# First units of a layer on unscaled x, their eviction scaled, and low halves moved to VectorE

## Time and profile before

| | |
|---|---|
| median of 3 runs | 1706.01 us (1705.09 to 1707.49) |
| the profiled execution | 1704.73 us |
| its span, first to last instruction | 1702.9 us |
| mean granted TensorE clock | 0.975 |
| TensorE busy | 1593.6 us, 94% |
| VectorE busy | 934.9 us, 55% |
| ScalarE busy | 855.7 us, 50% |
| GpSimd busy | 741.6 us, 44% |
| HBM traffic | 140 GB/s over the span |

### The profile page before, as it was taken

The page is one execution under the profiler, slowest core; times in us unless marked ns, Lnnn a source line. Parts: engine busy times, 40 slices in busy tenths (PEclk is TensorE's granted clock), DMA queues, the critical chain, the costliest instruction groups (busy, mean ns, idle before and its releaser), DMA issues.

```text
span 1702.9 us, 28287 instructions
## 1 busy us (share of the span) xinstructions
PE 1593.6 (94%) x10947; PEld 1454.9 (85%) x10947; DVE 934.9 (55%) x2023; ACT 855.7 (50%) x1526; POOL 741.6 (44%) x572
## 2 busy tenths in 40 slices
PE   4999878999999989999899988899999999889998
PEld 3888778998788989999888878898887778889998
DVE  3799965444565554444379998423035545633332
ACT  2577764553455444444357776443325646444442
POOL 0688853332222424444258895365411112334432
PEclk8999989999999999999999999999999999999999
DMA  4654435446553546766444434675752112646654
GB/s 127 143 146 135 130 108 175 133 165 127 122 123 124 163 135 177 195 175 197 124 124 137 136 128 138 152 186 140 182 153 71 51 56 86 194 136 177 187 156 125
DMA packets 341453, 240.11 MB, mean 141 GB/s; under 512 B 36925, under 2 KB 328475, under 8 KB 341320
## 3 DMA queue, kind: packets, MB, share of 16 engines
q1 hardware_dynamic: 329880, 231.33, 47.7%
q10 hardware_dynamic: 10992, 6.29, 1.7%
q0 software_dynamic: 448, 0.69, 0.5%
HBM read 236.55 MB, written 1.74 MB: 140 GB/s over the span
## 4 chain that ended last, share of the span: by engine, by line
PE 70%; DVE 17%; ACT 5%; issue 4%; POOL 2%; DMA 1%; SPq 1%; DVEq 0%; POOLq 0%; ACTq 0%
PE bank L598 8%; DVE bank L876 8%; PE bank L599 8%; PE bank L600 8%; PE bank L634 4%; PE bank L636 4%; PE bank L635 4%; PE bank L990 4%; PE bank L1288 3%; PE bank L596 3%; PE bank L1289 3%; PE bank L1290 3%; PE bank L610 2%; DVE wlo L371 2%; PE bank L1083 1%
## 5 line engine op out<-in xcount | busy, mean ns | idle before, releaser
L371 POOL TENSOR_TENSOR wlo<-ring,whi 128x1024 fp32r<-128x1024 f32 (+3 forms) x210 | 481.7, 2295 | 786.0 <-ACT whi L362 785.9
L362 ACT CAST whi<-ring 128x1024 fp32r<-128x1024 f32 (+4 forms) x389 | 379.2, 990 | 274.8 <-PE bank L600 106.2
L598 PE MATMUL bank<-xh,whi 128*128 128x256 f32 x1384 | 402.4, 291 | 32.4 <-DVE xl L562 19.4
L371 DVE TENSOR_TENSOR wlo<-ring,whi 128x1024 fp32r<-128x1024 f32 (+3 forms) x179 | 254.6, 1423 | 267.0 <-ACT whi L362 266.1
L599 PE MATMUL bank<-xl,whi 128*128 128x256 f32 x1384 | 397.0, 287 | 0.0
L600 PE MATMUL bank<-xh,wlo 128*128 128x256 f32 x1384 | 396.7, 287 | 0.0
L598 PEld LDWEIGHTS bank<-xh,whi 128*128 128x128 f32 x1384 | 271.2, 196 | 42.3 <-issue 39.8
L599 PEld LDWEIGHTS bank<-xl,whi 128*128 128x128 f32 x1384 | 271.6, 196 | 0.2
L600 PEld LDWEIGHTS bank<-xh,wlo 128*128 128x128 f32 x1384 | 271.2, 196 | 0.0
L819 POOL TENSOR_TENSOR scratch<-scratch 128x256 f32<-128x256 f32 x288 | 211.3, 766 | 127.0 <-ACT scratch L764 123.1
L596 PE MATMUL bank<-sqb,ring 128*128 128x256 f32 x1024 | 230.1, 385 | 17.3 <-DVE xl L562 9.7
(11 more groups left out here) (254 smaller groups left out, 2640.5 us busy)
## 6 DMA issues: line engine op xcount, KB each, us to landing
ring<-in_a_w_in_dram SPq DMA_DIRECT2D x64, 512.0 KB, 5.2
ring<-in_b_w_in_dram SPq DMA_DIRECT2D x32, 1024.0 KB, 5.8
ring<-in_c_w_in_dram SPq DMA_DIRECT2D x64, 512.0 KB, 5.4
ring<-in_w_in_dram SPq DMA_DIRECT2D x26, 1024.0 KB, 5.4
ring<-in_w_ffn_in_dram SPq DMA_DIRECT2D x44, 512.0 KB, 5.1
ring<-in_a_w_in_dram SPq DMA_DIRECT2D x16, 1024.0 KB, 5.3
ring<-in_a_w_out_dram SPq DMA_DIRECT2D x16, 1024.0 KB, 5.0
ring<-in_w_ffn_out_dram SPq DMA_DIRECT2D x16, 704.0 KB, 4.5
```

Source lines behind the costliest of these rows:

```text
L362: nc.scalar.copy(piece(whi, h)[:, :, 0:n], src).then_inc(hi_done, 1)
L371: engine.tensor_tensor(piece(wlo, h)[:, :, 0:n], src, piece(whi, h)[:, :, 0:n].bitcast(F32), ALU.subtract).then_inc(done, 1)
L598: nc.tensor.matmul(o, wh[:, k, :], xh[:, k, :], start=(k == 0), stop=False)
```

## The change

In each layer the first two projection units (in the forgetting attention the gate unit and the first quarter of query and key) are multiplied by x times gain, without the factor of the norm. ScalarE writes these halves (`raw_high`) for each group of x as soon as it is added, VectorE the low halves (`raw_low`), and `proj_raw` does the products, with the last sum of squares inside the first unit or behind it. VectorE multiplies the two banks by `rr` when it evicts them (`raw_scale`); later steps read that copy. The normalised `sqb`, `xh` and `xl` are made later, `xh` and `xl` over the unscaled ones when TensorE has read these (`norm_dve_all`, `norm_high`, `norm_low`), and the third unit waits for them. In the conformer layers GpSimd makes `sqb` from a copy `xg`, the first two val and gate units are no longer plain, and the first z unit is the first to need the normalised halves. The order of the first steps on VectorE and ScalarE changes with it. VectorE gets all low halves but those of z, of the first half of the conformer output, of the mixer projections from the third on, of the branches and the mix gates. At the very start ScalarE waits for the gains before its first weight halves.

```diff
-                halves.append((u, ap, k, n, dve and len(halves) % 2 == 0))
+                halves.append((u, ap, k, n, dve == ALL or (dve and len(halves) % 2 == 0)))
...
-        def plan_out(w, nk):
-
-            return [(kb, g, unit_in(w[kb * D:(kb + 1) * D, :], [(2 * g * P, 2 * P)], True))
+        def plan_out(w, nk, dve="all"):
+
+            return [(kb, g, unit_in(w[kb * D:(kb + 1) * D, :], [(2 * g * P, 2 * P)], dve if kb == 0 else ALL))
                     for kb in range(nk // KD) for g in range(4)]
 
...
+        def raw_high(act, ph, g):
+
+            act.wait_ge(x_done, 4 * ph + g + 1)
+            for k in (2 * g, 2 * g + 1):
+                if ph in (0, 3):
+                    nc.scalar.activation(xg[:, k, :], xT[:, k, :], ACT.Identity, scale=norm_g(GAIN[ph], k)).then_inc(xg_done, 1)
+                nc.scalar.activation(xh[:, k, :], xT[:, k, :], ACT.Identity, scale=norm_g(GAIN[ph], k)).then_inc(rh_done, 1)
+
+        def raw_low(dve, ph, g):
+            for k in (2 * g, 2 * g + 1):
+                dve.wait_ge(rh_done, KD * ph + k + 1)
+                nc.vector.scalar_tensor_tensor(xl[:, k, :], xT[:, k, :], norm_g(GAIN[ph], k), xh[:, k, :].bitcast(F32),
+                                               ALU.mult, ALU.subtract).then_inc(rl_done, 1)
+
+        def rr_both():
+            return rr[:, 0:S].unsqueeze(1).to_broadcast((P, 2, S))
...
         def rms_act(act, ph):
             for g in range(0 if ph == 0 else 3, 4):
+                raw_high(act, ph, g)
                 rms_square(act, ph, g)
             act.wait_ge(ss_done, ph + 1)
             nc.scalar.activation(std[:, 0:S], rms_bank[ph][:, 0:S], ACT.Sqrt, scale=1.0 / D, bias=eps).then_inc(std_done, 1)
-            for g in range(4):
-                act.wait_ge(xr_done, KD * ph + 2 * g + 2)
-                nc.scalar.copy(xh[:, 2 * g:2 * g + 2, :], sqb[:, 2 * g:2 * g + 2, :]).then_inc(xh_done, 1)
+
+        def norm_high(act, ph, g, u):
+
+            act.wait_ge(xr_done, KD * ph + 2 * g + 2)
+            if ph == 1:
+                act.wait_ge(half_done, u + 2 * g + 2)
+            elif g < 3:
+                act.wait_ge(raw_used, RAW_USED[ph] + g + 1)
+            else:
+                group_done(act, u)
+            nc.scalar.copy(xh[:, 2 * g:2 * g + 2, :], sqb[:, 2 * g:2 * g + 2, :]).then_inc(xh_done, 1)
+
+        def norm_low(dve, ph, g):
+            dve.wait_ge(xh_done, 4 * ph + g + 1)
+            nc.vector.tensor_tensor(xl[:, 2 * g:2 * g + 2, :], sqb[:, 2 * g:2 * g + 2, :],
+                                    xh[:, 2 * g:2 * g + 2, :].bitcast(F32), ALU.subtract).then_inc(xn_done, 1)
...
-        def rms_dve(dve, ph):
+        def rms_dve(dve, ph, lo=-1):
+            for g in range(0 if ph == 0 else 3, 4):
+                raw_low(dve, ph, g)
+            lo_dve_to(dve, lo)
             dve.wait_ge(std_done, ph + 1)
             nc.vector.reciprocal(rr[:, 0:S], std[:, 0:S]).then_inc(rr_done, 1)
             dve.wait_ge(rr_done, ph + 1)
-            def low(g):
-                dve.wait_ge(xh_done, 4 * ph + g + 1)
-                nc.vector.tensor_tensor(xl[:, 2 * g:2 * g + 2, :], sqb[:, 2 * g:2 * g + 2, :],
-                                        xh[:, 2 * g:2 * g + 2, :].bitcast(F32), ALU.subtract).then_inc(xn_done, 1)
-
+
+        def norm_dve_all(dve, ph):
             for k in range(KD):
                 nc.vector.scalar_tensor_tensor(sqb[:, k, :], xT[:, k, :], norm_g(GAIN[ph], k), rr[:, 0:S],
                                                ALU.mult, ALU.mult).then_inc(xr_done, 1)
-                if k % 2 == 1 and k >= 3:
-                    low(k // 2 - 1)
-            low(3)
+
+        def raw_scale(dve, ph, i, g, u, to):
+
+            group_done(dve, u)
+            nc.vector.tensor_tensor(to.rearrange("p (a t) -> p a t", t=S), bank[g % 2][:, :].rearrange("p (a t) -> p a t", t=S),
+                                    rr_both(), ALU.mult).then_inc(raw_ev, 1)
+
+        def raw_wait(eng, ph, i):
+            eng.wait_ge(raw_ev, RAW_EV[ph] + i + 1)
+
+        def proj_raw(pe, g, u, ph, opens=False, ends=False):
+
+            b = take_bank(pe, g)
+            for a, h in enumerate(hs(u)):
+                o = b[:, a * S:(a + 1) * S]
+                split_ready(pe, h)
+                wh, wl = piece(whi, h), piece(wlo, h)
+                for k in range(KD):
+                    if opens and a == 0:
+                        pe.wait_ge(rl_done, KD * ph + k + 1)
+                    nc.tensor.matmul(o, wh[:, k, :], xh[:, k, :], start=(k == 0), stop=False)
+                    nc.tensor.matmul(o, wh[:, k, :], xl[:, k, :], start=False, stop=False)
+                    mm = nc.tensor.matmul(o, wl[:, k, :], xh[:, k, :], start=False, stop=(k == KD - 1))
+                    if ends and h == last(u) and k in (1, 3, 5):
+                        mm.then_inc(raw_used, 1)
+                    if opens and a == 0 and k == KD - 3 and ph and len(hs(u)) > 1:
+                        rms_pe(pe, ph)
+                mm.then_inc(half_done, 1)
+                if opens and a == 0 and not (ph and len(hs(u)) > 1):
+                    rms_pe(pe, ph)
...
                 if kb == end:
+                    if g >= 1:
+                        raw_low(dve, n["ph"] + 1, g - 1)
                     group_done(dve, u)
...
+            pool.wait_ge(rr_done, n["ph"] + 1)
+            for k in range(KD):
+                pool.wait_ge(xg_done, KD * j + k + 1)
+                nc.gpsimd.tensor_tensor(sqb[:, k, :], xg[:, k, :], rr[:, 0:S], ALU.mult).then_inc(xr_done, 1)
...
+                        if c == 0 and k == TAPS_DVE // 4:
+                            raw_scale(dve, n["ph"], 1, *n["vg"][1], rawt(1))
...
+                if c == 1:
+                    for g in range(4):
+                        norm_low(dve, n["ph"], g)
...
+            g, u = n["f"]
+            dve_ahead(dve, u)
+            group_done(dve, u)
+            nc.vector.tensor_tensor(fw[:, 1, :], bank[g % 2][0:FH, 0:S], rr[0:FH, 0:S], ALU.mult).then_inc(raw_ev, 1)
+            norm_dve_all(dve, n["ph"])
...
                 dve_ahead(dve, u)
-                dve.wait_ge(c_cg, c + 1)
-                nc.vector.tensor_tensor(cup[:, c % 2, 2:S + 2], bank[g % 2][:, 0:S], ccg[:, c % 2, :], ALU.mult).then_inc(c_cu, 1)
+                if c:
+                    dve.wait_ge(c_cg, c)
+                    uu, cc = bank[g % 2][:, 0:S], ccg[:, c % 2, :]
+                else:
+                    raw_scale(dve, n["ph"], 0, g, u, craw[0])
+                    norm_dve_all(dve, n["ph"])
+                    raw_wait(dve, n["ph"], 0)
+                    uu, cc = craw[0][:, 0:S], craw[0][:, S:2 * S]
+                nc.vector.tensor_tensor(cup[:, c % 2, 2:S + 2], uu, cc, ALU.mult).then_inc(c_cu, 1)
...
                 dve_ahead(dve, u)
+                bb = bank[g % 2]
+                if c == 0:
+                    for i in range(4):
+                        norm_low(dve, n["ph"], i)
+                    raw_scale(dve, n["ph"], 1, g, u, craw[1])
+                    bb = craw[1]
...
+            lo_dve_to(dve, last(n["in"][1][2]))
+            for i in range(2):
+                _, g, u = n["in"][i]
+                if i == 1:
+                    norm_dve_all(dve, n["ph"])
+                group_done(dve, u)
+                nc.vector.tensor_tensor(qk[:, RAW_OF[i], :, :], bank[g % 2][:, :].rearrange("p (a t) -> p a t", t=S),
+                                        rr_both(), ALU.mult).then_inc(m_ev, 1)
+            for r in range(4):
+                norm_low(dve, n["ph"], r)
...
                 dve_ahead(dve, u)
+                src = bank[g % 2]
+                if i == 1:
+                    norm_dve_all(dve, n["ph"])
+                    for r in range(4):
+                        norm_low(dve, n["ph"], r)
+                if i < 2:
+                    raw_scale(dve, n["ph"], i, g, u, craw[i])
+                    src = craw[i]
                 dve.wait_ge(h_silu, i + 1)
-                nc.vector.tensor_tensor(y_slot(dve, n["y0"] + i), bank[g % 2][:, S:2 * S], sg[:, i % 2, :], ALU.mult).then_inc(y_raw, 1)
...
             act.wait_ge(set_pool, 1)
+            act.wait_ge(set_used, 1)
```

More of the change, by code:

```diff
@@ L290, in program @@
         first_half = []
+        ALL = "all"
         def cut(u, by_columns, dve, plain=False, rows_of=None):
@@ L428, in plan_conf @@
             for c in range(KE):
-                n["vg"].append((group((u_done, j * KE + c + 1)), unit_in(w, [(c * P, P), (E + c * P, P)], plain=True)))
+                n["vg"].append((group((u_done, j * KE + c + 1)), unit_in(w, [(c * P, P), (E + c * P, P)], c < 2 and ALL, plain=(c >= 2))))
                 if c % 4 == 3:
@@ L514, in plan_ffn @@
             n = {"ph": ph}
-            n["gu"] = [(group((y_raw, 64 + i + 1)), unit_in(w, [(i * P, P), (FF + i * P, P)], True)) for i in range(KF)]
+            n["gu"] = [(group((y_raw, 64 + i + 1)), unit_in(w, [(i * P, P), (FF + i * P, P)], ALL)) for i in range(KF)]
```

(10 more changed lines are left out.)

186 lines of the change are left out of this document (127 added, 59 removed).

## The result

The changed kernel takes 1714.53 us (median of 4 runs, 1711.99 to 1715.51). Against the kernel before the ratio is 1.0047, with a 95% interval of 1.0031 to 1.0063: some 8 us slower, where 12.4 us faster was forecast. The profiled execution took 1714.64 us.

The account below looks back on a forecast made before the run. TensorE, busy 94% of 1702.9 us, was taken to bound the kernel, VectorE's order setting the first conformer layer's pace. Terms 2.3 + 2.8 + 3.1 + 6.4 + 1.5 - 3.7 = 12.4 us off 1706.0 gave 1693.6, range 1684 to 1701.

Parts of the forecast that it names:

- The starts: Start of every layer: TensorE goes on with unscaled x times gain, no wait 2 to 7 us after the previous layer's outputs.
- What came late next: New waits: 4.7 us before unit 2 in the short layer, 4.1 in the feed-forward, 4.2 before L1288 in the forgetting layer.
- the short layer: Short convolution: unit 2 starts 18.2 instead of 21.3 us after the previous layer's last output matmul; less 0.8 for clock, +2.3.
- the feed-forward: Feed-forward: unit 2 starts 17.6 instead of 21.2 us after the previous layer's last output matmul; less 0.8 for clock, +2.8.
- The low halves of the weights: Moving weight low halves to VectorE brings nothing where TensorE is always busy: taken at 0, from -3 to +3 us.
- Rival (c): Late low halves in VectorE's blocked queue, short and feed-forward: 33 us lost, about 1727; in one only, about 1713; chance 0.10.
- The forgetting layer's head start: Forgetting attention: L1288 comes 3.9 us earlier after the gate unit; less 0.8 for the clock, +3.1 us.
- The mixer layer: Mixer layer: L610 starts 16.6 instead of 23.0 us after the previous layer's last output matmul, +6.4 us.
- The conformer layers: VectorE's tap chain sets the pace: first conformer layer -3.7 us (-2.1 to -5), second +1.5 us.
- a sign of being wrong: First conformer layer: ending more than 6 us later would show the forecast wrong.
- Rival (b): Conformer layers eat the gain: first loses 10 us instead of 3.7, second another 3; gain 3.1, about 1703; chance 0.11.

Follow-up runs that it names:

- Run 3: Kernel before the change with only the low halves moved to VectorE, without the new starts: 1715.49 us, ratio 1.0060.
- run 6: Changed kernel with only the forgetting layer's z and v weight low halves shared with GpSimd again, query/key ones left on VectorE: 1703.78 us, ratio 0.9993.
- run 7: Changed kernel with only VectorE's order altered in the last query/key group of the forgetting layer, scales and evictions ahead of look-ahead low halves: 1705.71 us, ratio 0.9993.
- run 5: Changed kernel with GpSimd's low halves of the mixer layer held back until VectorE's eight norm multiplies are done: 1711.83 us, ratio 1.0038.
- run 2: Changed kernel with the moved low halves shared with GpSimd again, except those of formerly plain first units and the 16-column gate unit: 1714.27 us, ratio 1.0056.
- run 8: Changed kernel with conformer starts as before, run 5's wait, run 7's order, and norm low parts ahead of the second look-ahead in short and feed-forward: 1687.15 us.
- runs 9 and 10: Run 8 with VectorE making all low halves in both conformer layers (1697.43 us), or only those of their first four z groups (1695.03 us).

## Why the prediction was wrong

**The starts: right.** Behind every layer TensorE goes on into the next one's first unit without a wait. Inside that unit one is left, of 1.99 us before the square sum at 862.04 in the second conformer layer, where the forecast had none in any layer. What came late next was named and nearly sized: 4.01 for 4.7 us in the short layer, 3.65 for 4.1 in the feed-forward, 4.03 for 4.2 in the forgetting layer. The short layer gained 2.55 for 2.3, the feed-forward 4.15 for 2.8. That the short layer came so near is in part luck: unit 2 came 4.1 us nearer to E (17.4 instead of 21.5), not 3.1, and the stretch at half clock behind it cost 1.7 us, not 0.8. In the feed-forward the head start was 4.85 us (17.05 instead of 21.9), where 3.6 had been worked out.

**The low halves of the weights: the step that failed.** "Where TensorE is busy all the time, an earlier low half brings nothing", "Taken at 0, from -3 to +3". I counted VectorE's load in the short layer and did not walk its queue through the last query/key group, where TensorE waits for what VectorE does (scales, evictions) and not only for low halves. Moving a half to VectorE put a blocking wait ahead of them. Run 3 puts 11.5 us on it, run 6 puts it on the z and v halves, run 7 on the order. Rival (c) had the mechanism, a queue held by a wait, and the wrong place: it looked for late low halves in the short and feed-forward layers, where none is late. That its figure for one of the two layers, about 1713, lies near the 1714.5 measured is chance: neither of these layers lost anything. Its chance of 0.10 was too small for a term that had not been walked through.

**The forgetting layer's head start: right in size, worth less than said.** 4.1 us at L1406, 0.4 us left 95 us later. I had taken off 0.8 for the clock; 1.7 went to it at once (0.50 from 304.7 to 308.1), and 1.5 to new waits for evictions, ended at 330.52, 357.76 and 385.02 (0.98, 0.27 and 0.27). What took the last 0.5 stays open.

**The mixer layer: a term missing.** L678 at E+19.5 instead of E+16.6, since the eight multiplies took 6.9 instead of 3.2 us beside GpSimd's low halves (run 5). I had applied that slowing to the conformer layers only. Of the 3.5 us that were gained (E+23.0 before), 1.7 went at once into a stretch at 0.50 right behind the new wait (1130.7 to 1134.1), and 1.4 into another of 6.8 us at 1185.3, where the kernel before shows 3.4 at 1174.2.

**The conformer layers: the terms mis-sized.** The timeline of the first held to 0.5 us up to channel 1. The sum behind it was wrong as it stood: -2.3, -2.8 to -3.9 and the 2.86 that the stall swallows give -2.2 to -3.3, not -2.1 to -5. Measured, the four low halves cost 4.0, just above the range given; the weight low half beside GpSimd's cost another 1.2, and those of z 1.5 to 2.1 more. For these last two 0.8 to 1.2 had been allowed in the second layer and nothing in the first, which ends 6.35 us later: the forecast had named more than 6 as a sign of being wrong. Rival (b) named these layers but for a reason that did not come: the scaled tiles were covered. GpSimd's multiplies (L891 in the page's list) took 0.92 us each where 0.73 was estimated; from the 0.40 and the ratio 2.40 to 1.22 it would have been 0.79.

**The cause of the slowing.** VectorE's taps read one tensor from SBUF and one from PSUM. In the changed kernel they take the same at all times, most of them beside GpSimd's adds (ns, shortest/median/longest):

```profile
L971 DVE SCALAR_TENSOR_TENSOR bank<-scratch,convw,bank x576: 473/482/486, 50.4 to 1030.0; 128x256 f32<-128x256 f32 x192
```

The instructions named above that take longer beside it each read two operands from SBUF: L605, L554, L580 (1.21 instead of 0.68) and L374. In run 2 the held one ends 0.28 us after GpSimd's. The Trainium skill, SBUF — State Buffer, section "Who interferes with whom", says as much: a VectorE instruction with two SBUF inputs contends with a GpSimd instruction that reads SBUF, and whoever issues first holds the shared ports for the whole instruction. By that rule L554, issued 0.15 us after GpSimd's low half, waits for its end and then runs its own 0.48 us: 2.47 - 0.15 + 0.48 = 2.8 us by this estimate, against 2.60 measured; the trace agrees to 0.2 us. That GpSimd's low halves are the cause is shown by run 5 (6.89 us became 3.25); that it hangs on the two operands in SBUF is read from comparing instructions and was not tested by a run.

## What to carry to other kernels

When work is moved to another engine, walk that engine's queue through every stage that the work reaches, the stage behind included, and ask of each blocking wait who stands behind it; a load that fits says nothing on that. Place look-ahead work behind the evictions and scales on which the bottleneck engine waits: in run 7 that alone was worth 8.5 us of one layer, at no instruction less. Before halving a stream of work with two inputs in SBUF between VectorE and GpSimd, measure the pair: where the two engines had nothing else to do, VectorE's half of a pair took 2.53 us (run 8, from 227.72) against 2 x 1.22 for both on VectorE, so that the split saved nothing; where GpSimd was adding taps anyway, it paid (runs 9 and 10).

## What was not expected of the hardware

I had expected an instruction beside GpSimd to take about twice as long, from the medians of the earlier trace rows; it takes about its own time and what is left of GpSimd's instruction. So the smaller one suffered more: 0.48 became 2.60 us, 1.22 became 2.4 to 2.5.

The place of the stretches at half clock moves a layer by 3 us without a change in its code: the mixer layer took 398.2 in the changed kernel and 394.8 in run 6. In both L678 starts at E+19.5 to 19.6. In run 6 a stretch of 3.4 us lies ahead of the wait before L678, which shrinks from 3.24 to 1.74 us by it, and in the changed kernel behind that wait, where it costs 1.7 us. Later, 74 us after E, the clock is at 0.50 for 6.8 us in the changed kernel and for 3.4 in run 6, which makes most of the rest. Whole kernels show it too: run 8 lost 0.022 x 1685.6 = 37 us of full clock, the change 51. Fewer waits of TensorE gave more than their own length: run 8 was expected at 1691 to 1695 and took 1687. What decides in which of two like places the clock falls was not settled here.
